# A decoder layer: k turned on VectorE instead of TensorE, x held back, and four steps moved in the order

## The chip, the cores and the metric

One core of a Trainium2 chip runs the whole program. The metric is the device time of one execution in microseconds. A core has TensorE (PE: products and transposes, which write PSUM), VectorE (DVE), ScalarE (ACT), GpSimd (POOL) and SyncE (SP). Each runs its own list of instructions in order, and they wait for each other by semaphores. SP, POOL and ACT can issue DMAs.

## The reference

One layer of a decoder with 512 prompt tokens and 32 sample tokens (8 sequences of 4). All is fp32.

```
h = rms_norm(x, g_pre);  z = h @ w_in                 # 1024 -> 3072 columns
q, k, v, ga, u, vs, gg = split(z)                     # 512, 256, 256, 512, 512, 512, 512
att = attend(q, k, v)          # prompt: causal attention; sample: the best past blocks of 256 keys
gm  = gelu(u) * (tril(w_sp) @ group_layer_norm(gelu(vs)) + b_sp)
y   = x + rms_norm(concat(att * silu(ga), gm * silu(gg)) @ w_out, g_post)
outputs: y, and the rows of k and v (token by token, 256 numbers each), prompt and sample
```

## The kernel before

Activations are held with channels on the partitions and tokens along the free dimension. The prompt's 512 tokens and the 32 sample tokens make five token tiles (four of 128, one of 32), columns 0 to 543 of `act_hi` and `act_lo`. Each fp32 factor is split into a high and a low part, and a product is the sum of hi x hi, lo x hi and hi x lo.

**Stages.** At the start the x tiles are loaded, normalised, turned on TensorE (`turn_x`) and split: ScalarE writes `act_hi` (semaphore `x_hi`), VectorE `act_lo` (`x_split`). The input projection then has 24 tiles of 128 columns, each in two halves over the tokens: 48 halves, numbered by h in `HALF_ORDER`. A half is 24 products. Its result lies in a Z bank until ScalarE or VectorE has taken it (step ZE). After half 47 come the sums for the output projection (MIX, Y, YS, Y2).

**The order.** `schedule()` (L82) writes one list by hand: half after half, and after each half the side steps that `after(h, ...)` has put there, in the order in which it was called. Every engine walks the same list and does its part of each step, so a step's place in the list is its place in every engine's queue. The steps of this case:

- WT and WB (L103, L104): the spatial weights turned, then one small product `rep` x `wspT`, for which VectorE writes `rep` in its part of WT (L1115).
- KVN (L100 to L102): k and v of a token tile, held as `kv32` (two tiles of k, two of v), turned on TensorE into a T bank (four turns, L1487), taken by ScalarE into `kvn`, and stored by POOL with two DMAs (L751, L752). v's part goes on into `v_st`.
- KTR: VectorE's 32x32 block transposes of the sample's cached K pages.
- VSN (L108, L116): the gelu'd `vs` turned, group sums and centring on VectorE, squares on ScalarE; LN and LNM finish the normalisation, LNM with a product on POOL.
- PSC, PN, PTR, PPV, ATT: one of 16 units of prompt attention (128 queries of a pair of heads): scores and maxima, exponentials and norms, turned probabilities, product with v, and the gate. Unit u starts after half 30 + u; PN is in the same half as PSC, PTR one half later, PPV and ATT two later.
- SP: the spatial product for a group pair, three of them after halves 43, 45 and 47 ahead of that half's PSC (L127).

**Banks.** Steps that turn something take the two T banks by turns; a step waits until the step two uses before has been read out (`bank_free`, L489). `pT_lo` on VectorE frees a bank of PTR, `vn` one of VSN, `sp_sum` one of SP.

**Queues.** SP issues x, the page table, one weight pair, K and V pages, `w_out` and the results. POOL issues the other weight pairs, `w_spatial`, the k and v stores, `g_sgu`, `b_spatial` and `g_post`, and between them computes half of the weights' low parts (`w_lo`, L696). `kv32` lies in the same memory as `zgg`, which VectorE writes from half 40 on (L1106).

Of the kernel before, what the change touches and what calls it, by code (L numbers as in the profile page):

```python
# [34 lines left out]
fp32 = mybir.dt.float32  # L35
# [7 lines left out]
P = 128  # L43
# [38 lines left out]
def schedule():  # L82

    s = [("XT", tt) for tt in range(TT)]
    side = {}

    def after(n, *steps):
        side.setdefault(n, []).extend(steps)


    for m, h in enumerate((3, 4, 5, 6, 10, 11, 12, 13, 15, 16, 17, 18, 21, 22, 23, 24)):
        after(h, ("KTR", m))
    after(6, ("WT",))
    after(7, ("WB",))
    after(9, ("DSC", 0), ("DSC", 1))
    after(12, ("KOW",))
    after(14, ("DSC", 2), ("DSC", 3), ("DOWN",))
    after(15, ("OWN",), ("DSM", 0))
    after(17, ("DEX", 0))
    after(16, ("KVN", 4), ("KVN", 0))  # L100
    for n, h in enumerate((17, 20, 22)):
        after(h, ("KVN", 1 + n))  # L102
    after(19, ("DPT", 0))  # L103
    after(20, ("DSC", 4), ("DSC", 5), ("DPV", 0, 0), ("DPV", 0, 1))  # L104
    after(22, ("DPV", 0, 2), ("DPV", 0, 3))
    after(24, ("DPV", 0, 4), ("DPV", 0, 5))
    after(28, ("DEX", 1))
    for n, h in enumerate((24, 25, 28, 29)):  # L108
        after(h, ("VSN", n))
    after(25, ("DSC", 6), ("DSC", 7), ("DPV", 0, 6), ("DPV", 0, 7))  # L110
    after(26, ("DOD", 0), ("DSM", 1))
    after(28, ("DOT", 0))
    after(30, ("DPT", 1))
    for pg in range(8):
        after(31 + pg // 2, ("DPV", 1, pg))
    after(31, ("VSN", 4))  # L116
    after(32, ("LN",))
    for n, tt in enumerate((4, 0, 1, 2, 3)):
        after(33 + 2 * n, ("LNM", tt))
    after(35, ("DOD", 1))  # L120
    after(36, ("DOT", 1))
    after(40, ("AS",))
    first = 30
    for h in range(first, 2 * NT):
        u = h - first
        if h in [2 * TILE_OF["gg", gp] + 3 for gp in range(3)]:
            after(h, ("SP", (h - 3) // 2 - TILE_OF["gg", 0]))  # L127
        if u < len(UNITS):
            after(h, ("PSC", u), ("PN", u))
        if 1 <= u < len(UNITS) + 1:  # L130
            after(h, ("PTR", u - 1))
        if 2 <= u < len(UNITS) + 2:
            after(h, ("PPV", u - 2))
# [13 lines left out]
    s += [("Y2", tt) for tt in Y_ORDER]  # L147
    return s
# [94 lines left out]
def build(nc, x_prompt, x_sample, cache_k, cache_v, page_table, g_pre, w_in, g_sgu, w_spatial,  # L243
# [8 lines left out]
    def kv_rows(prompt, sample, tt):  # L252
        if tt < 4:
            return prompt[0, 0, tokens(tt)].rearrange("s h d -> s (h d)")
        return sample[0].rearrange("b t h d -> (b t) (h d)")

    with ExitStack() as ctx:
        def sem(name):
            return ctx.enter_context(nc.semaphore(name))
# [9 lines left out]
        def place(name, shape, dt, at):  # L269
            return nc.alloc_sbuf_tensor_at(name, shape, dt, offset=at)  # L270
# [31 lines left out]
        y_sum = place("y_sum", [SMP, 2, 512], fp32, R_Q + 26624)  # L302

        R_V = region(4096 + 8192 + 10240)
        kvn = place("kvn", [P, 2, 512], fp32, R_V)
        ln_sq = place("ln_sq", [P, 512], fp32, R_V)
        g_sgu_bc = place("g_sgu_bc", [P, 512], fp32, R_V + 2048)
        w2_hi = place("w2_hi", [P, 2, D], f32r, R_V + 4096)
# [108 lines left out]
        k_in = [sem(f"k_in{n}") for n in range(4)]  # L417
        v_in = [sem(f"v_in{n}") for n in range(4)]

        stored_kv = [sem("stored_kv0"), sem("stored_kv1")]  # L420
        stored_kvs = sem("stored_kvs")
        stored, stored_sgu = sem("stored"), sem("stored_sgu")

# [142 lines left out]
        def _(sp):  # L566
# [86 lines left out]
            sp.wait_ge(stored, 16 * 2 * TT)  # L653
            sp.wait_ge(stored_sgu, 16)
            for n in range(2):
                sp.wait_ge(stored_kv[n], 2 * 32)
            sp.wait_ge(stored_kvs, 32)


# [1 line left out]
        def _(pool):  # L661
# [71 lines left out]
            for s in SCHEDULE:  # L733
                kind = s[0]
                if s == ("Z", TILE_OF["u", 0], 1):

                    pool.wait_ge(vst_done, 4)
                    pool.wait_ge(stored_kv[1], 2 * 32)
                    pool.dma_start(g_sgu_bc[:, :], g_sgu[0:1, :].broadcast_to([P, 512])).then_inc(gsgu_in, 16)
                elif kind == "Z" and next_split(*s[1:]) is not None:  # L740
                    n = next_split(*s[1:])
# [3 lines left out]
                        load_w_in((n + 3) // 2)  # L745
                elif kind == "KVN":
                    tt = s[1]
                    src = kvn[:, tt % 2, :] if tt < 4 else kv_s[:, :]
                    pool.wait_ge(t_free["act"], freed(T_FREED_BY, T_OF[s])[1])
                    landed = stored_kv[tt % 2] if tt < 4 else stored_kvs  # L750
                    pool.dma_start(kv_rows(k_prompt, k_sample, tt), src[:, 0:KVW]).then_inc(landed, 16)  # L751
                    pool.dma_start(kv_rows(v_prompt, v_sample, tt), src[:, KVW:2 * KVW]).then_inc(landed, 16)  # L752
                elif kind == "DOT" and s[1] == 1:

                    pool.wait_ge(dpv, 2 * PAGES)
# [25 lines left out]
        def _(act):  # L781
# [32 lines left out]
            for s in SCHEDULE:  # L814
# [72 lines left out]
                elif kind == "KVN":  # L887
                    n, tt = T_OF[s], s[1]
                    R = ROWS[tt]
                    if 2 <= tt < 4:  # L890
                        act.wait_ge(stored_kv[tt % 2], 32)
                        act.wait_ge(vst_done, tt - 1)
                    take(n, (kvn[:, tt % 2, :] if tt < 4 else kv_s[:, 0:512]), T[n % 2][0:R, :])
                    if tt < 4:
                        act.wait_ge(t_free["act"], freed(T_FREED_BY, n)[1])
                        nc.scalar.activation(v_st[:, tt, :, 0:HD], kvn[:, tt % 2, KVW:].rearrange("p (h d) -> p h d", h=KVH), ACT.Copy)\
                            .then_inc(vst_hi, 1)
                elif kind == "DEX":
                    r = s[1]
# [16 lines left out]
                elif kind == "VSN":  # L916
# [3 lines left out]
                    if tt:  # L920
                        act.wait_ge(ssq_done, tt)
                    else:
                        act.wait_ge(stored_kv[0], 2 * 32)
# [92 lines left out]
        def _(dve):  # L1016
# [32 lines left out]
            for s in SCHEDULE:  # L1049
# [19 lines left out]
                elif kind == "ZE":  # L1069
# [28 lines left out]
                    elif what in ("ga", "gg"):  # L1098
                        g = GATE_HALVES.index(h)
                        dst = zga if what == "ga" else zgg  # L1100
                        dve.wait_ge(z_hi, 12 + g + 1)
                        if g == 0:
                            dve.wait_ge(t_full, T_OF["VSN", 4] + 1)
                        if what == "gg" and j == 0 and half == 0:
                            dve.wait_ge(t_full, T_OF["KVN", 3] + 1)
                        nc.vector.scalar_tensor_tensor(dst[:, j, cols], th[:, g % 2, 0:wide], 1.0, bank[:, 0:wide], ALU.add, ALU.mult)\  # L1106
                            .then_inc(z_free["dve"], 1)
                elif kind == "WT":
# [8 lines left out]
                elif kind == "WB":  # L1117
# [3 lines left out]
                                            T[n % 2][0:SMP, 0:GRP * DEC_T].rearrange("p (g t) -> p g t", g=GRP).unsqueeze(2).broadcast_to([SMP, GRP, DEC_B, DEC_T]),  # L1121
                                            bd_mask[:, :, :].unsqueeze(1).broadcast_to([SMP, GRP, DEC_B, DEC_T]), ALU.mult)\
                        .then_inc(t_free["dve"], 1)
                elif kind == "KVN":
                    tt = s[1]
                    if tt < 4:
                        dve.wait_ge(vst_hi, tt + 1)
                        nc.vector.tensor_tensor(v_st[:, tt, :, HD:], kvn[:, tt % 2, KVW:].rearrange("p (h d) -> p h d", h=KVH),
                                                v_st[:, tt, :, 0:HD].bitcast(fp32), ALU.subtract).then_inc(vst_done, 1)
                elif kind == "KTR":  # L1130
                    m = s[1]
# [240 lines left out]
        def _(pe):  # L1372
# [47 lines left out]
            for s in SCHEDULE:  # L1420
# [4 lines left out]
                elif kind == "Z":  # L1425
# [6 lines left out]
                    if h < 3:  # L1432

                        pe.wait_ge(w_hi_done, t + 1)
                        pe.wait_ge(x_hi, 4)
                        if h == 2:
                            pe.wait_ge(xn_done, 2 * TT)
                        for k in range(KD):
                            mm(out, wh[:, k, :], act_hi[:, k, cols], start=(k == 0), stop=False)
                        if h == 1:  # L1440
                            turn_x(2)
# [254 lines left out]
```

## Time and profile before

| | us |
|---|---|
| median of three timed runs | 283.56 (283.49 to 284.8) |
| the profiled execution | 283.24 |
| its span in the trace | 281.5 |
| TensorE's products busy | 270.4 (96%) |
| VectorE busy | 197.4 (70%) |
| ScalarE busy | 154.9 (55%) |
| GpSimd busy | 81.5 (29%) |

Times in the trace count from the span's start. TensorE's granted clock is full (1.00, 2.4 GHz) until 275 us. Products are pipelined: a row shows one as 0.27 to 0.30 us long, but they start 0.12 to 0.13 us apart, so a wait is read from the idle time in brackets behind a row, or from the distance between starts. In a timeline row stand the start, the length of the group, engine, line, operation, out<-in, shapes, the count (xN), and the idle time of the engine before it with what ended it.

### The profile page before, as it was taken

Reading aid. Unit: us, or ns where it says so; the run is one execution under the profiler, and the core shown is the slowest. Engines: PE = TensorE matmul, PEld = TensorE weight load, DVE = VectorE, ACT = ScalarE, POOL = GpSimd, SP = SyncE. Lnnn points to the kernel's source line nnn. Section 1 sums busy time; section 2 is a strip of 40 time slices with the busy share of each in tenths; the row PEclk is TensorE's granted clock in tenths of the full one; section 3 lists DMA queues with packets and bytes.
Section 4 is the critical chain, followed back from the end, with each engine's and each line's share of the span. In section 5 each row is a group of like instructions: output and inputs, shape, how many; then the busy total and the mean of one; then the engine's idle time right before and its main releaser. Section 6 shows DMA issues by size and latency. Waiting matters only on the chain.

```text
span 281.5 us, 6112 instructions
## 1 busy us (share of the span) xinstructions
PE 270.4 (96%) x2155; PEld 237.5 (84%) x2155; DVE 197.4 (70%) x451; ACT 154.9 (55%) x355; POOL 81.5 (29%) x96
## 2 busy tenths in 40 slices
PE   8999999999999999999899999999899999999992
PEld 3799988999997887998787999998798976767892
DVE  4786885699743525835558889899979894927773
ACT  5973667632692323288875556555374563628621
POOL 4676505210412142243044373333350510000000
PEclk9999999999999999999999999999999999999998
DMA  7989994379999969530572017021008404040043
GB/s 246 332 270 196 207 282 114 125 206 232 265 313 283 318 190 311 152 122 31 149 242 68 2 29 234 1 81 71 0 2 275 193 1 149 2 150 2 19 175 123
DMA packets 29922, 43.39 MB, mean 154 GB/s; under 512 B 2963, under 2 KB 22419, under 8 KB 29892
## 3 DMA queue, kind: packets, MB, share of 16 engines
q1 hardware_dynamic: 26226, 29.76, 37.2%
q0 software_dynamic: 3664, 13.24, 15.0%
q8 instruction: 17, 0.28, 0.5%
q14 instruction: 13, 0.11, 0.1%
q10 hardware_dynamic: 2, 0.00, 0.0%
HBM read 39.59 MB, written 3.41 MB: 153 GB/s over the span
## 4 chain that ended last, share of the span: by engine, by line
PE 72%; DVE 14%; ACT 9%; issue 3%; DVEq 0%; POOL 0%; ACTq 0%; POOLq 0%
PE Z L1459 11%; PE Z L1464 10%; PE Z L1460 10%; PE T L1377 3%; DVE probs L1258 3%; PE S L1501 3%; PE Z L1415 2%; DVE pT_lo L1264 2%; PE O L1600 2%; PE O L1536 2%; PE S L1415 2%; PE S L1416 2%; PE Z L1417 2%; PE S L1417 2%; PE Z L1416 2%
## 5 line engine op out<-in xcount | busy, mean ns | idle before, releaser
L1459 PE MATMUL Z<-act_hi,w_hi 128*128 128x288 f32 (+1 forms) x344 | 89.5, 293 | 0.4 <-ACT zvs L873 0.3
L1460 PE MATMUL Z<-act_lo,w_hi 128*128 128x288 f32 (+1 forms) x344 | 88.0, 288 | 0.0
L1459 PEld LDWEIGHTS Z<-act_hi,w_hi 128*128 128x128 f32 x344 | 64.8, 188 | 2.6 <-issue 1.6
L1460 PEld LDWEIGHTS Z<-act_lo,w_hi 128*128 128x128 f32 x344 | 64.8, 188 | 0.0
L696 POOL TENSOR_TENSOR w_lo<-w_raw,w_hi 128x1024 fp32r<-128x1024 f32 x16 | 38.2, 2388 | 54.4 <-ACT w_hi L796 54.4
L1464 PE MATMUL Z<-act_hi,w_lo 128*128 128x256 f32 (+1 forms) x336 | 49.0, 288 | 0.0
L1464 PEld LDWEIGHTS Z<-act_hi,w_lo 128*128 128x128 f32 x336 | 44.8, 188 | 0.0
L796 ACT ACTIVATE w_hi<-w_raw 128x1024 fp32r<-128x1024 f32 x32 | 33.5, 1051 | 15.0 <-DMA w_raw<-in_w_out 10.0
L940 ACT ACTIVATE probs<-S,nmax 128x128 f32<-128x128 f32 (+3 forms) x32 | 16.6, 524 | 23.9 <-DVE nmax L1248 22.5
L1027 DVE TENSOR_TENSOR w_lo<-w_raw,w_hi 128x1024 fp32r<-128x1024 f32 x15 | 18.1, 1209 | 16.0 <-ACT w_hi L796 16.0
L1135 DVE STREAM_TRANSPOSE kT<-k_ring 128x1024 f32<-128x1024 f32 x16 | 19.7, 1238 | 0.4 <-PE S L1501 0.2
L704 POOL DMA_DIRECT2D w_raw<-in_w_in x10 | 9.3, 928 | 33.2 <-DVE w_lo L1027 29.7
L1258 DVE TENSOR_SCALAR probs<-probs,rsum 128x128 f32<-128x128 f32 (+3 forms) x32 | 15.2, 475 | 1.1
L1248 DVE TENSOR_REDUCE nmax<-S 128x1 f32<-128x128 f32 (+3 forms) x32 | 14.1, 480 | 1.2 <-PE S L1576 1.1
L1264 DVE TENSOR_TENSOR pT_lo<-T,pT_hi 128x128 fp32r<-128x128 f32 (+3 forms) x32 | 14.1, 482 | 0.1
L1377 PE MATMUL T<-ident,probs 128*128 128x128 f32 x80 | 12.1, 276 | 2.1 <-DVE vn L1227 0.9
L952 ACT ACTIVATE pT_hi<-T 128x128 fp32r<-128x128 f32 (+3 forms) x32 | 12.2, 440 | 0.0
L768 POOL TENSOR_TENSOR vn<-vn,g_sgu_bc 128x512 f32<-128x512 f32 (+1 forms) x5 | 6.4, 1285 | 19.4 <-DVE vn L1240 19.4
L1600 PE MATMUL O<-pT_hi,v_st 128*128 128x256 f32 x40 | 11.5, 315 | 0.5 <-DVE zga L1278 0.5
L777 POOL TENSOR_TENSOR zu<-zu,zgg 128x544 f32<-128x544 f32 x4 | 5.4, 1352 | 22.0 <-DVE zgg L1106 22.0
L882 ACT ACTIVATE th<-Z 128x256 f32<-128x256 f32 (+1 forms) x16 | 6.4, 399 | 9.7 <-PE Z L1464 9.5
L1255 DVE RECIPROCAL rsum<-psums 128x1 f32<-128x1 f32 x32 | 5.1, 160 | 8.9 <-ACT probs L940 8.9
(272 smaller groups left out, 557.3 us busy)
## 6 DMA issues: line engine op xcount, KB each, us to landing
w_raw<-in_w_in POOLq DMA_DIRECT2D x10, 1024.0 KB, 7.0
k_ring<-in_cache_k SPq DMA_DIRECT2D x64, 128.0 KB, 4.7
v_ring<-in_cache_v SPq DMA_DIRECT2D x64, 128.0 KB, 4.0
w_raw<-in_w_out SPq DMA_DIRECT2D x8, 512.0 KB, 4.4
x_sb<-in_x_prompt SPq DMA_DIRECT2D x4, 512.0 KB, 5.6
x_res<-in_x_prompt SPq DMA_DIRECT2D x4, 512.0 KB, 5.2
out<-y_sb SPq DMA_DIRECT2D x8, 256.0 KB, 2.0
w_raw<-in_w_in SPq DMA_DIRECT2D x2, 512.0 KB, 6.5
```

What stands on the lines that cost most here:

```text
L696: nc.gpsimd.tensor_tensor(w_split_tile(False, n), w_tile(n), w_split_tile(True, n).bitcast(fp32), ALU.subtract)\
L796: nc.scalar.activation(w_split_tile(True, n), w_tile(n), ACT.Copy).then_inc(w_hi_done, 1)
L940: ins = nc.scalar.activation(probs[:, u % 2, g, 0:keys], S[:, g * 512:g * 512 + keys], ACT.Exp, bias=nmax[:, u % 2, g:g + 1], accum_out=ps ...
L1027: nc.vector.tensor_tensor(w_split_tile(False, n), w_tile(n), w_split_tile(True, n).bitcast(fp32), ALU.subtract)\
L1135: nc.vector.transpose(kT[:, m // 2 % 2, m % 2, :, :, :].rearrange("p q a j -> p (q a j)"), k_slot(m).rearrange("p q c -> p (q c)")).then_i ...
L1258: nc.vector.tensor_scalar(part, part, rsum[:, u % 2, g:g + 1], 0.5, ALU.mult, ALU.mult).then_inc(p_norm, 1)
L1264: nc.vector.tensor_tensor(pT_lo[:, u % 2, 0:blocks, g, :], T[(n + g) % 2][:, 0:blocks * P].rearrange("p (j q) -> p j q", q=P), pT_hi[:, u ...
L1377: return nc.tensor.transpose(T[n % 2][0:out_rows, col:col + rows], in_, ident[0:rows, 0:rows])
L1459: mm(out, wh[:, k, :], act_hi[:, k, cols], start=(k == 0), stop=False)
L1460: mm(out, wh[:, k, :], act_lo[:, k, cols], start=False, stop=False)
L1464: last = mm(out, wl[:, k, :], act_hi[:, k, cols], start=False, stop=(k == KD - 1))
L1600: last = mm(O[o_bank(u)][:, 0:256], v_st[:, j, kvh, :], part[:, u % 2, j, :, :].rearrange("p g q -> p (g q)"), start=(j == 0 and e == 0), ...
```

## The change

- k of the four full token tiles is no longer turned on TensorE. In new steps KTB (after halves 22 and 23) VectorE transposes 32x32 blocks of the two k tiles in place; in KTD (after halves 34 and 35) POOL stores them with four DMAs each, in pieces of 32 numbers. VectorE's first write of `zgg` waits for these eight stores. v is still turned on TensorE, two turns for each full tile, and has a smaller tile `vn_t` of its own; the 32-token tile is as before.
- SP waits for x tile 1 before it issues x tiles 2 to 4 and what follows.
- The first products of halves 0 to 2 wait for three writes of `act_hi`, the fifth product for four.
- WB moves from half 7 to 8; VSN 2, 3, 4 from halves 28, 29, 31 to 27, 28, 29; in half 43 SP 0 goes behind PSC, and PPV ahead of PTR.
- With `kvn` gone from its memory, the load of `g_sgu` waits for nothing.

```diff
@@ schedule()
-    after(7, ("WB",))
+    after(8, ("WB",))
...
+    for j in range(2):
+        after(22 + j, ("KTB", j))
+        after(34 + j, ("KTD", j))
...
-    for n, h in enumerate((24, 25, 28, 29)):
+    for n, h in enumerate((24, 25, 27, 28)):
         after(h, ("VSN", n))
...
-    after(31, ("VSN", 4))
+    after(29, ("VSN", 4))
...
-        if h in [2 * TILE_OF["gg", gp] + 3 for gp in range(3)]:
-            after(h, ("SP", (h - 3) // 2 - TILE_OF["gg", 0]))
-        if u < len(UNITS):
-            after(h, ("PSC", u), ("PN", u))
...
+        spread = [gp for gp in range(3) if h == 2 * TILE_OF["gg", gp] + 3]
+        if spread and spread != [0]:
+            after(h, ("SP", spread[0]))
+        if spread == [0]:
+            after(h, ("PSC", u), ("SP", 0), ("PN", u), ("PPV", u - 2), ("PTR", u - 1))
+        else:
+            if u < len(UNITS):
+                after(h, ("PSC", u), ("PN", u))
...
@@ tiles and semaphores
-        kvn = place("kvn", [P, 2, 512], fp32, R_V)
+        vn_t = place("vn_t", [P, 2, KVW], fp32, R_V)
...
-        stored_kv = [sem("stored_kv0"), sem("stored_kv1")]
+        stored_v = [sem("stored_v0"), sem("stored_v1")]
+        stored_k, k_turned = sem("stored_k"), sem("k_turned")
@@ SP
             load_first(1)
+            sp.wait_ge(x_in[1], 16)
             for tt in (2, 3, 4):
                 sp.dma_start(x_sb[0:ROWS[tt], tt, :], x_src[tt]).then_inc(x_in[tt], 16)
@@ POOL
                 if s == ("Z", TILE_OF["u", 0], 1):
-                    pool.wait_ge(vst_done, 4)
-                    pool.wait_ge(stored_kv[1], 2 * 32)
                     pool.dma_start(g_sgu_bc[:, :], g_sgu[0:1, :].broadcast_to([P, 512])).then_inc(gsgu_in, 16)
...
+                    if tt < 4:
+                        pool.dma_start(kv_rows(v_prompt, v_sample, tt), vn_t[:, tt % 2, :]).then_inc(stored_v[tt % 2], 16)
+                    else:
+                        pool.dma_start(kv_rows(k_prompt, k_sample, tt), kv_s[:, 0:KVW]).then_inc(stored_kvs, 16)
+                        pool.dma_start(kv_rows(v_prompt, v_sample, tt), kv_s[:, KVW:2 * KVW]).then_inc(stored_kvs, 16)
+                elif kind == "KTD":
+                    j = s[1]
+                    rows = k_prompt[0, 0].rearrange("(b j) h d -> j b (h d)", j=32)
+                    pool.wait_ge(k_turned, j + 1)
+                    for a in range(4):
+                        at = P * j + 32 * a
+                        pool.dma_start(rows[:, :, at:at + 32], kv32[32 * a:32 * a + 32, j, 0:SEQ].rearrange("p (b i) -> p b i", i=32))\
+                            .then_inc(stored_k, 16)
@@ ScalarE
                     if 2 <= tt < 4:
-                        act.wait_ge(stored_kv[tt % 2], 32)
+                        act.wait_ge(stored_v[tt % 2], 16)
...
+                    if tt < 4:
+                        take(n, vn_t[:, tt % 2, :], T[n % 2][:, 0:KVW])
...
@@ VectorE
                         if what == "gg" and j == 0 and half == 0:
                             dve.wait_ge(t_full, T_OF["KVN", 3] + 1)
+                            dve.wait_ge(stored_k, 8 * 16)
...
+                elif kind == "KTB":
+                    j = s[1]
+                    dve.wait_ge(k_first, 2 * j + 2)
+                    nc.vector.transpose(kv32[:, j, 0:SEQ], kv32[:, j, 0:SEQ]).then_inc(k_turned, 1)
@@ TensorE
-                        pe.wait_ge(x_hi, 4)
...
                         for k in range(KD):
+                            if k % 4 == 0:
+                                pe.wait_ge(x_hi, 3 + k // 4)
                             mm(out, wh[:, k, :], act_hi[:, k, cols], start=(k == 0), stop=False)
...
-                    for j in range(4):
-                        last = turn(n, j * P, kv32[:, j, tokens(tt)], P, ROWS[tt])
+                    for j in range(4) if tt == 4 else (2, 3):
+                        last = turn(n, (j if tt == 4 else j - 2) * P, kv32[:, j, tokens(tt)], P, ROWS[tt])
```

## Rows read from the trace of the kernel before

**Rows 1.** TensorE's and others' busy time in one stretch; engine, us (instructions), clock, DMA.
```profile
165.00:203.00 38.00, 36.61 (x297) 34.45 (x295) 34.20 (x90) 21.23 (x59) 15.82 (x12) 1.00 0.24 77
```

**Rows 2.** Waits of TensorE; line waited for releaser: us in total, times, longest.
```profile
PE T L1377 <- DVE pT_lo L1264: 0.6, 1, 0.6
...
PE T L1610 <- DVE pT_lo L1264: 0.6, 1, 0.6
...
PE O L1600 <- DVE zga L1278: 0.5, 1, 0.5
```

**Rows 3.** Timeline at the start: start us, us, engine, line; and landings of x_sb.
```profile
9.43 1.07 ACT L824 ACTIVATE act_hi<-O 128x512 fp32r<-128x512 f32 x2
...
10.05 1.29 DVE L1059 TENSOR_TENSOR act_lo<-O,act_hi 128x512 fp32r<-128x512 f32 x2
...
10.65 1.18 PE L1439 MATMUL Z<-act_hi,w_hi 128*128 128x256 f32 x8 [0.54 <-ACT act_hi L824]
...
11.34 1.07 ACT L801 ACTIVATE x_sq<-x_sb 128x1024 f32<-128x1024 f32 x1
...
DMA to landing us min/median/max: 3.3/7.0/8.0
```

**Rows 4.** Timeline around WB, VectorE then TensorE.
```profile
38.63 0.17 DVE L1115 COPY rep<-ident 4x32 f32<-4x32 f32 x1
...
38.90 0.21 PE L1479 MATMUL T<-wspT,rep 4*32 4x32 f32 x2 [0.50 <-issue]
```

**Rows 5.** Timeline of TensorE, four turns and then two.
```profile
120.60 0.60 PE L1377 MATMUL T<-ident,zvs 128*128 128x128 f32 x4
...
121.04 0.38 PE L1377 MATMUL T<-ident,od 128*128 128x128 f32 x2
```

**Rows 6.** Groups of the page (count | busy, mean ns); timeline of VectorE.
```profile
L1135 DVE STREAM_TRANSPOSE kT<-k_ring 128x1024 f32<-128x1024 f32 x16 | 19.7, 1238 | 0.4 <-PE S L1501 0.2
...
104.78 0.69 DVE L1225 TENSOR_REDUCE ln_mu<-T 128x8 f32<-128x512 f32 x1 [4.98 <-PE T L1377]
```

**Rows 7.** Timeline, unit 0's second turn on TensorE and a VSN sum on VectorE.
```profile
136.09 0.30 PE L1377 MATMUL T<-ident,probs 128*128 128x128 f32 x1 [0.85 <-DVE vn L1227]
...
121.24 0.69 DVE L1225 TENSOR_REDUCE ln_mu<-T 128x8 f32<-128x512 f32 x1 [2.34 <-PE T L1377]
```

**Rows 8.** Timeline at half 43, VectorE twice, then TensorE.
```profile
202.63 0.68 DVE L1285 TENSOR_TENSOR sp_sum<-T,b_bc 128x512 f32<-128x512 f32 x1
...
203.96 0.75 DVE L1248 TENSOR_REDUCE nmax<-S 128x1 f32<-128x256 f32 x2
...
203.46 0.30 PE L1377 MATMUL T<-ident,probs 128*128 128x128 f32 x1 [0.60 <-DVE sp_sum L1285]
```

**Rows 9.** Timeline of POOL, halves 34 to 36.
```profile
153.35 2.37 POOL L696 TENSOR_TENSOR w_lo<-w_raw,w_hi 128x1024 fp32r<-128x1024 f32 x1 [2.05 <-ACT w_hi L796]
...
163.33 2.38 POOL L696 TENSOR_TENSOR w_lo<-w_raw,w_hi 128x1024 fp32r<-128x1024 f32 x1 [2.46 <-ACT w_hi L796]
...
166.27 0.94 POOL L704 DMA_DIRECT2D w_raw<-in_w_in  x1 [0.56 <-POOL w_lo L696]
...
167.20 1.25 POOL L757 DMA_DIRECT2D b_bc<-in_b_spatial  x2
```

**Rows 10.** Timeline of VectorE, three products of probs.
```profile
166.66 0.70 DVE L1258 TENSOR_SCALAR probs<-probs,rsum 128x384 f32<-128x384 f32 x1
...
188.20 0.42 DVE L1258 TENSOR_SCALAR probs<-probs,rsum 128x384 f32<-128x384 f32 x1
...
197.91 1.90 DVE L1258 TENSOR_SCALAR probs<-probs,rsum 128x128 f32<-128x128 f32 x1
```

**Rows 11.** DMA queues of the page; VectorE's first zgg in the timeline.
```profile
q1 hardware_dynamic: 26226, 29.76, 37.2%
...
q0 software_dynamic: 3664, 13.24, 15.0%
...
189.76 0.41 DVE L1106 SCALAR_TENSOR_TENSOR zgg<-th,Z 128x256 f32<-128x256 f32 x1
```

More of the change, by code:

```diff
@@ L125, in schedule @@
         u = h - first
-        if h in [2 * TILE_OF["gg", gp] + 3 for gp in range(3)]:
-            after(h, ("SP", (h - 3) // 2 - TILE_OF["gg", 0]))
-        if u < len(UNITS):
-            after(h, ("PSC", u), ("PN", u))
[L130 to L133, printed above, removed]
+        spread = [gp for gp in range(3) if h == 2 * TILE_OF["gg", gp] + 3]
[6 more added lines that the diff above has]
+                after(h, ("PSC", u), ("PN", u))
+            if 1 <= u < len(UNITS) + 1:
+                after(h, ("PTR", u - 1))
+            if 2 <= u < len(UNITS) + 2:
+                after(h, ("PPV", u - 2))
         after(h, ("ZE", h // 2, h % 2))
@@ L655, in _ @@
             for n in range(2):
-                sp.wait_ge(stored_kv[n], 2 * 32)
+                sp.wait_ge(stored_v[n], 2 * 16)
+            sp.wait_ge(stored_k, 8 * 16)
             sp.wait_ge(stored_kvs, 32)
@@ L747, in _ @@
                     tt = s[1]
-                    src = kvn[:, tt % 2, :] if tt < 4 else kv_s[:, :]
                     pool.wait_ge(t_free["act"], freed(T_FREED_BY, T_OF[s])[1])
-                    landed = stored_kv[tt % 2] if tt < 4 else stored_kvs
-                    pool.dma_start(kv_rows(k_prompt, k_sample, tt), src[:, 0:KVW]).then_inc(landed, 16)
-                    pool.dma_start(kv_rows(v_prompt, v_sample, tt), src[:, KVW:2 * KVW]).then_inc(landed, 16)
+                    if tt < 4:
[11 more added lines that the diff above has]
+                            .then_inc(stored_k, 16)
                 elif kind == "DOT" and s[1] == 1:
@@ L890, in _ @@
                     if 2 <= tt < 4:
-                        act.wait_ge(stored_kv[tt % 2], 32)
+                        act.wait_ge(stored_v[tt % 2], 16)
                         act.wait_ge(vst_done, tt - 1)
-                    take(n, (kvn[:, tt % 2, :] if tt < 4 else kv_s[:, 0:512]), T[n % 2][0:R, :])
+                    if tt < 4:
+                        take(n, vn_t[:, tt % 2, :], T[n % 2][:, 0:KVW])
+                    else:
+                        take(n, kv_s[:, 0:512], T[n % 2][0:R, :])
                     if tt < 4:
                         act.wait_ge(t_free["act"], freed(T_FREED_BY, n)[1])
-                        nc.scalar.activation(v_st[:, tt, :, 0:HD], kvn[:, tt % 2, KVW:].rearrange("p (h d) -> p h d", h=KVH), ACT.Copy)\
+                        nc.scalar.activation(v_st[:, tt, :, 0:HD], vn_t[:, tt % 2, :].rearrange("p (h d) -> p h d", h=KVH), ACT.Copy)\
                             .then_inc(vst_hi, 1)
@@ L922, in _ @@
                     else:
-                        act.wait_ge(stored_kv[0], 2 * 32)
+                        for n in range(2):
+                            act.wait_ge(stored_v[n], 2 * 16)
+                        act.wait_ge(vst_done, 4)
                     nc.scalar.activation(ln_sq[0:R, :], vn[0:R, tt, :], ACT.Square).then_inc(sq_done, 1)
@@ L1127, in _ @@
                         dve.wait_ge(vst_hi, tt + 1)
-                        nc.vector.tensor_tensor(v_st[:, tt, :, HD:], kvn[:, tt % 2, KVW:].rearrange("p (h d) -> p h d", h=KVH),
+                        nc.vector.tensor_tensor(v_st[:, tt, :, HD:], vn_t[:, tt % 2, :].rearrange("p (h d) -> p h d", h=KVH),
                                                 v_st[:, tt, :, 0:HD].bitcast(fp32), ALU.subtract).then_inc(vst_done, 1)
```

## The prediction

> **What bounds the kernel now.** I read the page's busy table first, then TensorE's waits, then the timeline at each wait. TensorE is the busiest engine, and its products follow each other without a break almost everywhere, so a microsecond of work or waiting taken from its queue is worth a microsecond unless something later waits anyway. The exception is halves 36 to 43: there VectorE is busy 34.20 of 38.00 us [rows 1], and two of TensorE's waits near 194 to 203 us, 0.6 us each, end on a T bank that VectorE's `pT_lo` still reads [rows 2]. In that stretch VectorE falls behind by about a unit and TensorE pays for it at its end. The reader is to see two regimes: a TensorE queue with a handful of holes, and one stretch where the hole's size is VectorE's lag.
>
> **The change, part by part.** All clock times are those of the profiled execution, 283.24 us long with a span of 281.5.
>
> *Start.* The first products wait for four `act_hi` writes; now the first four wait for three. The pair of writes runs from 9.43 for 1.07 us, so the third ends near 9.97; TensorE started at 10.65, 0.15 after the fourth ended at 10.50 [rows 3]. So the first product starts at about 10.12. But the second pass needs `act_lo`, which ends at 10.05 + 1.29 = 11.34 [rows 3]; with the same 0.15 that is 11.49, and it began near 10.65 + 1.03 = 11.68 (eight products in about 1.03 us before the next pass). Gain 0.2 us; bounds 0 and 0.5.
>
> *x held back.* SP now waits until x tile 1 has landed before it issues tiles 2 to 4, the page table and the second weight pair. Behind that wait in SP's queue stand all the K pages and everything later. ScalarE reads tile 2 at 11.34, straight after its own earlier work [rows 3]; the loads of x took 3.3 to 8.0 us from issue to landing [rows 3]. The two weight tiles stand ahead of x tile 2 in the queue either way, so I cost it at nothing; the cover is ScalarE's earlier work. Bounds: a gain of 0.2 (x tile 1 a little earlier) and a loss of 1.5, worked out below.
>
> *WB from half 7 to 8.* Its product waited for `rep`, which VectorE wrote at 38.63 for 0.17; TensorE stood idle 0.50 us before 38.90 [rows 4]. After half 8 `rep` is 2 us old. The next things due are the bank of half 6 and the second split, both done before 37. Gain 0.5 to 0.65; I take 0.6.
>
> *Eight turns leave TensorE.* Four full tiles need two turns each instead of four. Four turns take from 120.60 to 121.04, 0.44 us [rows 5]; four such pairs are 4 x 0.22 = 0.88 us, bounds 0.7 and 1.0. The turned copy on ScalarE halves too, off the path.
>
> *KTB on VectorE.* Two block turns of 128x512. Sixteen of 128x1024 took 1238 ns on average [rows 6]; half the columns cost 0.62 to 1.24 us, nearest 0.65. They come at halves 22 and 23, in front of the 4.98 us that VectorE idled before 104.78 [rows 6]: 1.3 us hidden. Without that cover they would cost 1.3.
>
> *Centring (VSN) at 27, 28, 29.* The transposes of unit 0 waited 0.85 us at 136.09 for the T bank that VSN 4 held [rows 7]. VSN 4 now runs two halves earlier, and that bank is long free. VSN 2 goes into the 2.34 us that VectorE idled before 121.24 [rows 7]; what follows it there keeps its order. About 2 us of VectorE and 0.6 of ScalarE also leave the stretch before unit 1's maxima, so `nmax` of units 1 and 2 comes sooner, and of the 0.5 us that O waited for `zga` [rows 2] I count 0.3. Gain 1.15; bounds 0.6 (VSN 4's old place taken by a wait for ScalarE's table loads) and 1.6.
>
> *SP 0 inside half 43.* Before, SP's sum (202.63, 0.68) and product stood ahead of unit 13's maxima (203.96) on VectorE, and TensorE's second turn of unit 12 waited 0.60 to 203.46 for that sum [rows 8]. Now the maxima go first: 0.67 us (two in 0.75, overlapping), so the sum ends near 204.0 and the turn waits until about 204.05. But PPV 11, 1.0 us of TensorE work that stood behind this turn, is now ahead of it. The next half starts 0.4 us sooner. Bounds -0.3 and 0.9.
>
> *k stored in 128-byte pieces.* Eight POOL DMAs of 512 pieces. One of 1024 pieces holds POOL for 0.94, two of 256 for 1.25 together [rows 9]; 512 lie between 0.63 and 0.94, nearest 0.72: 5.8 us. POOL is free from 153.35 + 2.37 = 155.7 to 163.33 [rows 9], 7.6 us in which only one 1.3 us `vn` product lies; queued behind are that product, the next `w_lo` (not needed before half 38) and a weight pair. Hidden on POOL. On VectorE not quite: a `probs` product of 384 columns took 0.70 us beside POOL's DMA issues and 0.42 at 188.20 without them [rows 10]. Six such VectorE instructions at +0.2 are 1.2 us; VectorE waits some 0.75 us for TensorE in these halves, so 0.4 is carried into the VectorE-bound stretch. Bounds 0 and 1.4.
>
> The page "SBUF — State Buffer" of the Trainium skill (section "Who interferes with whom") says that VectorE in a two-port mode and GpSimd lock each other out for a whole instruction. The 128-column `probs` at 197.91 agrees: 1.90 us, ending about when POOL's instructions do [rows 10]. By the rule each of the eight issues could block a VectorE instruction for its full length, which is a rival below; the 0.28 us above speaks for less.
>
> *The new wait for stored_k.* VectorE's first `zgg` (189.76 [rows 11]) waits for all eight stores; behind it stand every later step of VectorE, and through the T banks TensorE. 4096 pieces over 16 engines are 256 each. The mean packet of the SP queue took 0.372 x 16 x 281.5 / 26226 = 64 ns, that of POOL's 0.150 x 16 x 281.5 / 3664 = 184 ns [rows 11]. A piece between nothing and 184 ns makes 0 to 47 us from 155.7; nearest is the smaller packet: at most 16 us, so landed by 174. No cost; what hides it is the 34 us until 189.76.
>
> The page "DMA: Bandwidth & Descriptors" (section "Specifications") says that below 512 bytes a transfer is read, modified and written. No run here shows a piece of 128 bytes; if it doubled the 64 ns, the sum would stay as it is.
>
> **Sum.** 0.2 + 0.6 + 0.88 + 1.15 + 0.4 - 0.4 = 2.83 us; 283.24 - 2.83 = 280.4. The profiled run lies 0.3 under the median of the three timed runs (283.56), so this is 280.4 to 280.7; I say 280.4, since three bounds are wider towards gain.
>
> **Rivals.**
> *VectorE keeps what TensorE is given.* The lag in halves 36 to 43 is VectorE's own; if its units don't start earlier by what TensorE gains after half 30, the 1.15 and 0.4 come back as longer holes at 194 to 203. For it: 90% busy there [rows 1]. Against: VectorE enters the stretch waiting for TensorE, and VSN 4 leaves it. Time 283.24 - 1.68 + 0.4 = 282.0.
> *The lock in full.* Each of six VectorE instructions waits half an issue, 0.36: 2.2 us, less the 0.75 of slack: 1.4 instead of 0.4. Time 281.4.
> *x tile 2 comes late.* If it takes 8.0 us again, from an issue near 5.5 (x tile 1 landed), ScalarE reads it at 13.5 and not 11.34: 2.2 late, 0.7 of it slack; 1.5 lost, and the 0.2: 282.1. Against: it stood behind the same weights before.
> *The pieces are slow (the other side).* If a piece costs as much as a POOL packet, 184 ns, the stores end at 155.7 + 47 = 203, `zgg` is 13 us late and with it TensorE: 293. It decides from (189.76 - 155.7) / 256 = 133 ns a piece. For it: nothing so small is in the trace. Against: the smaller packets at 64 ns carry eight times the bytes.
> *The holes only move.* Another wait takes the place of WB's and VSN's: only the turns and the start remain, 282.2.
>
> **How the numbers follow.** Forecast 0.64 (its own range 279.2 to 281.6); VectorE keeps it 0.15; lock 0.07; late x 0.05; slow pieces 0.05; holes move 0.04. The best ends together (0.5 + 0.65 + 1.0 + 1.6 + 0.9) give 278.6. The range 278.8 to 282.2 leaves out slow pieces and a little at both edges. A measurement tells about 0.5%, 1.42 us, from no change, so faster means under 282.14: the forecast and the lock, most of the cases at 282.0 to 282.2 half and half: faster 0.82, same 0.13, slower 0.05.
>
> **What would show it.** No idle before `T<-wspT,rep`; two turns per full tile (twelve of kv, not twenty); the turns of unit 0 without a wait; TensorE's first product near 10.1; `zgg` not waiting on a DMA; half 44 some 2.8 us earlier; `probs` under 0.8 us beside the new DMA issues. It would be wrong if the holes at 194 to 203 grow by over a microsecond, if `zgg` waits for a store, or if ScalarE waits for x.

## The result, and the profile after

The changed kernel takes 280.91 us (median of six runs, 280.67 to 281.67) against 283.69 (283.49 to 285.0) beside it: a ratio of 0.9895 [0.9871, 0.9918], 2.78 us. The forecast was 280.4, range 278.8 to 282.2.

The profiled run of the changed kernel took 281.54 us (span 279.8) and lies above its own median, while that of before (283.24) lies below its own. So the two spans differ by 1.70 only. Cutting both traces at the starts of halves shows why (us from one start to the next, read on TensorE):

| from start to start | before | after | gained |
|---|---|---|---|
| span's start to half 3 (start) | 21.79 | 22.59 | -0.80 |
| 3 to 14 (WB) | 37.80 | 37.33 | 0.47 |
| 14 to 23 (KVN) | 37.24 | 36.35 | 0.89 |
| 23 to 34 (VSN) | 52.27 | 51.24 | 1.03 |
| 34 to 37 (KTD) | 16.59 | 16.84 | -0.25 |
| 37 to 42 | 25.13 | 25.11 | 0.02 |
| 42 to 44 (SP 0) | 13.79 | 13.38 | 0.41 |
| 44 to the end | 76.91 | 76.97 | -0.06 |

From half 3 to the end it is 259.73 and 257.22: 2.51 gained. This part hardly varies: in four kernels whose order behind half 3 is the same (the changed one, and the first, second and last of the experiments) it is 257.22, 257.31, 257.25 and 257.24. The start does vary: a run's time less 1.73 (what lies around the span) less this part gives half 3 at 21.7 to 22.7 in the six runs of the changed kernel, and at 22.0 to 23.5 in those of before. Effects of some tenths are therefore read below from half 3 on, in one trace each, and medians stand beside them. One execution of e3, 284.49 us, lies over 1.5% above that kernel's fastest and is left out of its row in the table of the experiments.

TensorE's waits after, the same view as [rows 2] (line, releaser: us in total, times, longest):

```profile
PE S L1431 <- DVE xn L1062: 1.4, 1, 1.4
PE T L1404 <- DVE sp_sum L1312: 0.9, 1, 0.9
PE T L1404 <- DVE pT_lo L1291: 0.6, 1, 0.6
PE T L1404 <- DVE vn L1254: 0.5, 1, 0.5
...
PE T L1404 <- DVE q_s L1243: 0.2, 1, 0.2
```

Of [rows 2], one wait on `pT_lo` and that on `zga` are gone; those on `vn` and `q_s` are new places, and the first is the start:

```profile
4.89 1.06 ACT L818 ACTIVATE x_sq<-x_sb 128x1024 f32<-128x1024 f32 x1 [1.73 <-DMA x_sb<-in_x_prompt]
...
7.31 0.66 PE L1431 MATMUL S<-ident,xn 128*128 128x128 f32 x4 [1.39 <-DVE xn L1062]
...
10.10 1.08 ACT L841 ACTIVATE act_hi<-O 128x512 fp32r<-128x512 f32 x2
...
10.84 0.36 PE L1467 MATMUL Z<-act_hi,w_hi 128*128 128x256 f32 x1
```

ScalarE first read x tile 0 at 4.89, at 4.16 before, though SP issued it at 0.82 in both and the change begins behind that issue. TensorE's first product is at 10.84, not at 10.1. Its place behind the writes of `act_hi` is the one that was meant: it starts 0.34 ahead of the end of the fourth write (11.18), where before it came 0.15 behind it. The writes themselves came 0.67 later than before.

WB (TensorE) has lost its wait:

```profile
41.94 0.24 PE L1507 MATMUL T<-wspT,rep 4*32 4x32 f32 x2
```

The k path, by the tile `kv` and its stores (count: shortest/median/longest ns; then the landing of the stores in us):

```profile
L1404 PE MATMUL T<-ident,kv x12: 270/272/273, 71.2 to 95.1; 128*128 128x128 f32 x8, 128*32 128x128 f32 x4
L768 POOL DMA_DIRECT2D out<-kv x8: 648/651/668, 154.1 to 158.6; - x8
...
L1150 DVE STREAM_TRANSPOSE kv<-kv x2: 669/686/703, 96.7 to 98.4; 128x512 f32<-128x512 f32 x2
...
DMA to landing us min/median/max: 2.1/2.2/3.5
```
```profile
188.36 0.41 DVE L1129 SCALAR_TENSOR_TENSOR zgg<-th,Z 128x256 f32<-128x256 f32 x1
```

Twelve turns, two block turns of 0.69 us, eight issues of 0.65, all landed before 163; `zgg` comes at 188.36 and waits for none. What the issues displace (POOL, then VectorE, then TensorE, answering [rows 9, 10]):

```profile
154.09 5.16 POOL L768 DMA_DIRECT2D out<-kv  x8
159.26 1.31 POOL L785 TENSOR_TENSOR vn<-vn,g_sgu_bc 128x512 f32<-128x512 f32 x1
```
```profile
154.08 0.29 DVE L1285 TENSOR_SCALAR probs<-probs,rsum 128x128 f32<-128x128 f32 x1
...
154.48 0.31 DVE L1285 TENSOR_SCALAR probs<-probs,rsum 128x128 f32<-128x128 f32 x1
...
157.24 0.68 DVE L1267 TENSOR_TENSOR vn<-vn,ln_rstd 128x512 f32<-128x512 f32 x1
...
159.76 0.97 DVE L1285 TENSOR_SCALAR probs<-probs,rsum 128x256 f32<-128x256 f32 x1
...
162.84 0.84 DVE L1243 COPY q_s<-T 64x32 f32<-64x32 f32 x4
```
```profile
163.83 0.41 PE L1404 MATMUL T<-ident,probs 128*128 128x128 f32 x2 [0.20 <-DVE q_s L1243]
```

The reader is to see that `probs` beside the issues is as short as ever (0.29, 0.31), that POOL's `vn` product, whose data VectorE finished at 157.92, starts at 159.26 behind the stores (1.34 us later; before it was 0.09), and that the `probs` which now meets it takes 0.97. The other product of that size, at 160.84, takes 0.35. `q_s` is then late and TensorE waits.

The centring (ScalarE, VectorE, TensorE, answering [rows 7]):

```profile
122.86 2.18 ACT L926 ACTIVATE pd<-S,bbias 128x128 f32<-128x128 f32 x8
...
125.09 0.68 ACT L946 ACTIVATE ln_sq<-vn 128x512 f32<-128x512 f32 x1
```
```profile
125.80 0.69 DVE L1257 TENSOR_REDUCE ln_var<-ln_sq 128x8 f32<-128x512 f32 x1 [3.28 <-ACT ln_sq L946]
...
127.98 0.67 DVE L1254 SCALAR_TENSOR_TENSOR vn<-ln_mu,T 32x512 f32<-32x512 f32 x1
```
```profile
128.71 0.66 PE L1404 MATMUL T<-ident,pd 128*128 128x128 f32 x4 [0.55 <-DVE vn L1254]
```

The 0.85 at 136.09 and the 0.5 at `zga` are gone. In their place ScalarE's square for VSN 3 stands behind eight exponentials, VectorE's variance waits 3.28 us for it, VSN 4's centring comes behind that, and TensorE waits 0.55 for the bank. SP 0 (VectorE, then TensorE, answering [rows 8]):

```profile
201.22 0.75 DVE L1275 TENSOR_REDUCE nmax<-S 128x1 f32<-128x256 f32 x2
201.89 0.68 DVE L1312 TENSOR_TENSOR sp_sum<-T,b_bc 128x512 f32<-128x512 f32 x1
```
```profile
202.71 0.30 PE L1404 MATMUL T<-ident,probs 128*128 128x128 f32 x1 [0.91 <-DVE sp_sum L1312]
```

One wait of 0.91 stands where two of 0.60 stood.

### The profile page after: what moved, and what is told of

The parts are those of the page before. It is cut to its first block, busy times and chain, and to the rows that moved or that the text cites. A ratio compares the mean times of both kernels' runs of the same rounds, so it can differ in the third digit from the quotient of the medians.

```text
span 279.8 us, 6103 instructions
## 1 busy us (share of the span) xinstructions
PE 269.2 (96%) x2147; PEld 236.6 (85%) x2147; DVE 199.0 (71%) x453; ACT 154.1 (55%) x355; POOL 84.3 (30%) x100
## 3 DMA queue, kind: packets, MB, share of 16 engines
q0 software_dynamic: 3728, 13.24, 15.3%
## 4 chain that ended last, share of the span: by engine, by line
PE 70%; DVE 16%; ACT 7%; issue 3%; DMA 1%; DVEq 0%; ACTq 0%
PE Z L1487 11%; PE Z L1492 10%; PE Z L1488 10%; PE T L1404 3%; DVE probs L1285 3%; PE O L1564 3%; PE S L1529 3%; PE Z L1442 2%; DVE pT_lo L1291 2%; PE S L1442 2%; PE S L1443 2%; PE Z L1444 2%; PE S L1444 2%; PE Z L1443 2%; PE O L1628 2%
## 5 line engine op out<-in xcount | busy, mean ns | idle before, releaser
L794 POOL TENSOR_TENSOR zu<-zu,zgg 128x544 f32<-128x544 f32 x4 | 5.4, 1356 | 21.7 <-DVE zgg L1129 21.7
```

## The experiments

All are edits of the changed kernel unless the text says otherwise; "from half 3" is from the start of half 3 to the end of the span.

| run | from half 3 | median (lowest to highest) | ratio to before |
|---|---|---|---|
| changed kernel | 257.22 | 280.91 (280.67 to 281.67) | 0.9895 [0.9871, 0.9918] |
| e1 no hold | 257.31 | 281.08 (280.69 to 282.85) | 0.9899 [0.9878, 0.9920] |
| e2 no split | 257.25 | 281.84 (281.01 to 282.02) | 0.9916 [0.9894, 0.9938] |
| e3 stores behind vn | 256.72 | 280.35 (280.07 to 281.80) | 0.9870 [0.9848, 0.9891] |
| e4 VSN 3 first | 257.05 | 280.54 (280.45 to 280.78) | 0.9882 [0.9863, 0.9902] |
| e5 k alone | 259.24 | 283.11 (282.60 to 285.23) | 0.9976 [0.9951, 1.0000] |
| e6 SP 0 old | 257.44 | 281.71 (281.57 to 283.61) | 0.9931 [0.9905, 0.9958] |
| e7 VSN old | 258.25 | 282.47 (281.63 to 285.07) | 0.9954 [0.9928, 0.9981] |
| e8 AS at 41 | 255.78 | 280.43 (279.30 to 282.35) | 0.9881 [0.9841, 0.9921] |
| e9 three orders | 255.34 | 279.81 (279.50 to 280.79) | 0.9851 [0.9823, 0.9879] |
| e10 w_lo first | 255.19 | 278.92 (278.60 to 280.46) | 0.9824 [0.9792, 0.9857] |
| e11 LN at 33 | 255.34 | 279.56 (278.88 to 281.62) | 0.9851 [0.9815, 0.9887] |
| e12 hold longer | 257.24 | 280.97 (280.79 to 281.36) | 0.9884 [0.9851, 0.9917] |

**The start: e1, e2, e12.**

```diff
-            sp.wait_ge(x_in[1], 16)
```


> The changed kernel, but SP no longer waits for x tile 1 before it issues tiles 2 to 4. In the profiled run of the changed kernel TensorE's first product began at 10.84 us and half 3 at 22.59, 11.75 later; before it was 10.65 and 21.79, 11.14 apart. Theory A (the hold costs nothing; x tile 0 merely landed later in that one run): 280.9 us within 0.3, and the distance stays 11.5 to 11.8. Theory B (the hold makes x tiles 2 and 3 late, and TensorE waits for them inside halves 0 to 2): the distance falls to about 11.1 and the time to 280.3. Theory C (the hold gives tiles 0 and 1 the road and so starts TensorE earlier): 281.4 or more.

```diff
-                            if k % 4 == 0:
-                                pe.wait_ge(x_hi, 3 + k // 4)
+                            if k == 0:
+                                pe.wait_ge(x_hi, 4)
```


> The changed kernel, but the first products of halves 0 to 2 wait for all four writes of act_hi again. Theory A (as predicted: the earlier first product is worth 0.2 us): 281.1. Theory B (the second pass waits for act_lo anyway, so the early start only opens a hole behind it): 280.9, the distance from the first product to half 3 shorter by what the first product starts later (0.2 to 0.5), half 3 where it was.

```diff
             sp.wait_ge(x_in[1], 16)
+            sp.wait_ge(w_first[0], 16)
```


> The changed kernel, but SP holds x tiles 2 to 4 until the first weight tile has landed as well (a larger dose of the same hold). In the changed kernel tiles 2 and 3 were issued from 6.31 us and ScalarE read tile 2 at 12.01 without a wait for it; ScalarE reads the first weight tile at 9.16. Theory A (the hold has slack, as predicted: ScalarE's earlier work covers it): ScalarE's read of x tile 2 waits at most 0.5 us, 280.7 to 281.2. Theory B (the rival in which x tile 2 comes late, priced at 1.5 us): issued near 8 us, x tile 2 is read at 13 or later, half 3 starts 1 to 2 us later than the 21.7 to 22.0 of undelayed starts, 281.9 or more.

e1 is theory A by its time (281.08); its profiled start was itself late (half 3 at 23.78, the distance 12.74, which no theory had); there ScalarE waited 0.73 us for x tile 2 without any hold. The larger dose is the clearer run:

```profile
7.65 0.82 SPq L628 DMA_DIRECT2D x_sb<-in_x_prompt  x2
...
11.64 1.07 ACT L819 ACTIVATE x_sq<-x_sb 128x1024 f32<-128x1024 f32 x1
```

Tiles 2 and 3 are issued at 7.65, in the kernel before from 2.83, and ScalarE still reads tile 2 at 11.64 with no wait: theory A. The x loads took 4.3 us at the median there, 7.0 in [rows 3]: issued later, they landed sooner behind their issue. The hold is free, and within these runs it gains nothing. In some traces ScalarE did wait for x tile 2, with the hold (0.41 in e6) and without it (0.36 in e5, 0.73 in e1), so such a wait is not the mark of the hold.

e2's median is 0.9 over the changed kernel, its lowest run 0.34; since a start varies by more than that, the times don't settle the split. The traces do, if they are read from the end of the fourth write of `act_hi`, which comes earlier or later with the loads. First e2, then e4 with the split (ScalarE, then TensorE):

```profile
9.57 1.07 ACT L841 ACTIVATE act_hi<-O 128x512 fp32r<-128x512 f32 x2
...
10.79 1.18 PE L1467 MATMUL Z<-act_hi,w_hi 128*128 128x256 f32 x8 [0.53 <-ACT act_hi L841]
...
13.71 1.12 PE L1467 MATMUL Z<-act_hi,w_hi 128*128 128x256 f32 x8
```
```profile
9.59 1.08 ACT L841 ACTIVATE act_hi<-O 128x512 fp32r<-128x512 f32 x2
...
10.32 1.18 PE L1467 MATMUL Z<-act_hi,w_hi 128*128 128x256 f32 x8
11.55 1.22 PE L1474 MATMUL Z<-act_lo,w_hi 128*128 128x256 f32 x8
12.61 1.11 PE L1477 MATMUL Z<-act_hi,w_lo 128*128 128x256 f32 x8
13.56 1.12 PE L1467 MATMUL Z<-act_hi,w_hi 128*128 128x256 f32 x8
```

From the end of the fourth write to the start of half 1 it is 3.07 us in e2 (10.64 to 13.71) and 2.89 in e4 (10.67 to 13.56). The three traces without the split have 3.06 or 3.07, the eleven with it 2.89 to 2.95. So the split gives about 0.17 by half 1: theory A, near its 0.2. The first product gains half a microsecond against that write, and most of it goes again in the wait for `act_lo`. Where ScalarE waits for no later x tile (before, e4, e7, e8, e12), halves 1 and 2 take 8.22 to 8.25 with or without the split, so half 3 keeps 0.13 to 0.16; in a late start it can't be told.

**The stores: e3, e5.** In e3, KTD is registered behind LNM:

```diff
-        after(34 + j, ("KTD", j))
...
         after(33 + 2 * n, ("LNM", tt))
+    for j in range(2):
+        after(34 + j, ("KTD", j))
```


> The changed kernel, but in half 35 POOL's vn product comes ahead of the second four k stores. Before, vn stood at 159.58 for 1.28 us and VectorE's probs of unit 5 came behind it (161.34, 0.35 us). In the changed kernel vn starts at 159.26, behind eight stores, 1.3 us after its data, and the 256-column probs beside it takes 0.97; TensorE then waits 0.35 at 163.5 for q_s. Theory A (the lag comes from the late vn product, not from the issues of the stores): vn near 158 again, probs 0.35 beside the second four stores, the wait for q_s gone, 280.6 (0.25 to 0.35 less). Theory B (VectorE is held by POOL's DMA issues themselves, 0.2 us each time): probs stays near 0.6 to 0.97 beside the stores, 280.9.

```profile
154.84 2.60 POOL L769 DMA_DIRECT2D out<-kv  x4
158.76 1.28 POOL L786 TENSOR_TENSOR vn<-vn,g_sgu_bc 128x512 f32<-128x512 f32 x1 [1.32 <-DVE vn L1268]
159.99 2.60 POOL L769 DMA_DIRECT2D out<-kv  x4
```
```profile
160.52 0.35 DVE L1286 TENSOR_SCALAR probs<-probs,rsum 128x256 f32<-128x256 f32 x1
...
160.98 0.44 DVE L1286 TENSOR_SCALAR probs<-probs,rsum 128x256 f32<-128x256 f32 x1
```

Theory A: beside four issues `probs` takes 0.35 and 0.44, and the stage from half 34 to 37 takes 16.63, 0.21 less; another 0.29 comes in half 42, 0.50 from half 3 on.

e5 is the kernel before with the k edits alone (the diff in the section on the change, without the start, WB, VSN and SP 0).

> The kernel before with the k change alone: two turns instead of four for each full token tile, KTB on VectorE, KTD on POOL; the start, WB, VSN and SP 0 as before. From the start of half 3 to the end the kernel before takes 259.73 us. Theory A (the terms add): eight turns less give 0.88, the vn product that the stores push into probs takes 0.24 back: 259.1 us from half 3, and 0.6 us under the time of before. Theory B (VectorE keeps what TensorE is given: the holes at 194 to 203 grow by as much): 259.5 to 259.7, and no difference that can be told.

Theory A by its stages: 36.39 against 37.24 from half 14 to 23 (0.85 gained), 16.80 against 16.59 from 34 to 37 (0.21 lost), none of it kept by VectorE later. The sum, 0.49, is under the 0.63 expected, because the stage of WB, which it doesn't touch, took 0.17 more in this trace: with WB in its old place TensorE waits again, 0.62 this time.

**The centring: e7, e4.**

```diff
-    for n, h in enumerate((24, 25, 27, 28)):
+    for n, h in enumerate((24, 25, 28, 29)):
...
-    after(29, ("VSN", 4))
+    after(31, ("VSN", 4))
```


> The changed kernel with VSN 2, 3, 4 back at halves 28, 29, 31. Theory A (the holes at 136.09 and 147.8 come back, the new one at 127.9 goes): 257.22 + 1.03 = 258.25 us from half 3, and about 1.0 over the changed kernel. Theory B (without them something else of ScalarE's table loads was the limit, so that less comes back): 257.5 to 257.8.

258.25: theory A. In e4, `after(28, ("DEX", 1))`, the step with the eight exponentials, stands behind the loop that places VSN.

> The changed kernel, but at half 28 VSN 3 stands ahead of DEX 1, so that ScalarE squares vn before its table load and the eight exponentials. In the changed kernel TensorE waits 0.55 us at 128.71 for VSN 4's centred vn (127.98), which VectorE makes only after VSN 3's variance (125.80, waiting 3.28 us for ScalarE's square behind the exponentials). Theory A (that queue order is the cause of the new hole): variance near 123.5, the hole at 127.9 shrinks from 0.82 to about 0.36, 280.4 to 280.5. Theory B (the exponentials become late instead, 0.7 us later, and TensorE waits for them at the first turns of the probabilities, 127.57): 280.9 or more.

```profile
121.77 0.64 ACT L946 ACTIVATE ln_sq<-vn 128x512 f32<-128x512 f32 x1 [1.00 <-DVE vn L1254]
```
```profile
145.98 0.36 PE L1628 MATMUL O<-pT_hi,v_st 128*128 128x256 f32 x1 [0.46 <-DVE zga L1305]
```

The cause is as theory A says: from half 3 on half 31 starts 0.74 earlier. But half 34 keeps 0.20 of that, for the wait on `zga` of [rows 2] is back (0.46): the next limit is the chain behind it. I had not named this third outcome.

**SP 0: e6.** The old order of half 43.

```diff
-        if spread and spread != [0]:
+        if spread:
             after(h, ("SP", spread[0]))
-        if spread == [0]:
-            after(h, ("PSC", u), ("SP", 0), ("PN", u), ("PPV", u - 2), ("PTR", u - 1))
-        else:
+        if True:
```


> The changed kernel with SP 0 and PPV of half 43 in the old order. The changed kernel takes 257.22 us from half 3 to the end. Theory A (as predicted, 0.4): 257.6, with two waits of TensorE (0.6 each) instead of one of 0.9. Theory B (both orders only place the same lag of VectorE): 257.2.

From half 42 to 44 it takes 13.77 against 13.38, 0.39: theory A at its place. From half 3 on only 0.22 is left: 0.08 lies behind half 44, which takes 76.90 there and 76.98 here, and the rest is some hundredths in other stages.

**What holds VectorE: e8, e10, and the better versions.**

```diff
-    after(40, ("AS",))
+    after(41, ("AS",))
```


> The changed kernel with AS (a product of 128x128 on VectorE) after half 41 instead of 40. In the changed kernel it takes 2.06 us at 183.25, beside POOL's w_lo (182.78 to 185.16); its like takes 0.29. TensorE's holes at 192.98 (0.87) and 201.53 (1.18) both end on a T bank that VectorE frees late. Theory A (VectorE's lag, made by such holds, sets the holes): AS takes about 0.3 in its new place, VectorE is up to 1.7 us earlier at half 41, the hole at 193 goes, and 256.0 to 256.6 us from half 3, 280.0 to 280.3 in all. Theory B (the hold only moves: w_lo holds the next product of probs instead): 257.2 and 280.9.

First the changed kernel, then e8: POOL's and VectorE's timeline, and a stretch of about halves 37 to 43 (columns as in [rows 1]):

```profile
182.78 2.38 POOL L706 TENSOR_TENSOR w_lo<-w_raw,w_hi 128x1024 fp32r<-128x1024 f32 x1 [1.87 <-ACT w_hi L813]
...
183.25 2.06 DVE L1333 TENSOR_TENSOR zga<-zga,q_s 128x128 f32<-128x128 f32 x1
```
```profile
163.40:201.40 38.00, 37.15 (x304) 35.27 (x302) 34.16 (x91) 21.23 (x59) 15.81 (x12) 1.00 0.25 77
```
```profile
187.85 0.28 DVE L1333 TENSOR_TENSOR zga<-zga,q_s 128x128 f32<-128x128 f32 x1
```
```profile
164.00:200.00 36.00, 35.90 (x298) 34.33 (x296) 32.02 (x89) 21.34 (x62) 15.09 (x11) 1.00 0.25 81
```

Theory A, and beyond it: 255.78, 1.44 less. The hole at 193 is gone and TensorE is busy 35.90 of 36.00. One 128x128 product had cost VectorE 1.8 us, and that was most of its lag at this hole. VectorE's busy share is about as before (32.02 of 36.00, 34.16 of 38.00): the share of [rows 1] didn't show what made the hole. The median falls by 0.48 only: three of the six runs took 281.2 or more, and none of these was traced. The medians of e9 to e11, which have the same move, lie 1.1 to 2.0 under the changed kernel. e9 is e3, e4 and e8 together.

> The changed kernel with three orders of the runs so far together: the second four k stores behind the vn product, VSN 3 ahead of DEX 1, AS after half 41. From half 3 to the end these gave 0.49, 0.17 and 1.44 us apart. Theory A (each shortens a hole of its own): 257.22 - 2.1 = 255.1. Theory B (0.29 of the first lay in the hole at 193 that the third takes away): 255.4. With a start of 21.7 to 22.0 that is 278.6 to 279.1 in all.

255.34: theory B; part of e3's gain lay in the hole that e8 takes away. e10 adds to e9:

```diff
-                    if lo_by(n) == "pool":
+                    if lo_by(n) == "pool" and n != TILE_OF["gg", 0] + 2:
                         split_lo(n)
...
                 elif kind == "ZE" and ORDER[s[1]][0] == "gg" and s[2] == 1:
                     j = ORDER[s[1]][1]
+                    if j == 0:
+                        split_lo(s[1] + 2)
```


> As the kernel with the three orders, but POOL makes the w_lo of the third gg tile ahead of its product zu<-zu,zgg of the first, not behind it. In the changed kernel with AS at 41 that w_lo ran from 193.70 to 196.10 and VectorE's 128-column probs beside it took 1.89 us (194.30), its like 0.29; w_hi was ready at 192.41. Theory A (the hold ends with POOL's instruction): w_lo ends near 194.8, probs takes about 0.6, VectorE is 1.2 us earlier at SP 0, TensorE's last hole in that stretch (0.86, on sp_sum) goes: 0.7 us less than with the three orders alone. Theory B (another probs is held instead, or zu comes late for SP 0): no less.

```profile
192.46 2.39 POOL L707 TENSOR_TENSOR w_lo<-w_raw,w_hi 128x1024 fp32r<-128x1024 f32 x1 [3.20 <-ACT w_hi L816]
194.81 1.36 POOL L797 TENSOR_TENSOR zu<-zu,zgg 128x544 f32<-128x544 f32 x1
```
```profile
194.26 0.67 DVE L1288 TENSOR_SCALAR probs<-probs,rsum 128x128 f32<-128x128 f32 x1
...
195.04 1.22 DVE L1288 TENSOR_SCALAR probs<-probs,rsum 128x128 f32<-128x128 f32 x1
```

Both theories in part: the first `probs` ends with `w_lo`, but the second is now held until `zu` ends (196.17). 0.15 less from half 3 on, not 0.7. e11 adds to e10 `after(33, ("LN",))` in place of 32.

> As the kernel before it, and LN (two table loads on ScalarE and two reciprocals on VectorE) after half 33 instead of 32. With VSN 3 first, TensorE waited 0.46 us at 145.98 for zga, behind a chain of ScalarE's table loads in which LN takes 137.94 to 139.56 and a load at 140.69; ScalarE sits idle 2.54 us at 144.6. Theory A (LN is what makes that chain late): the wait goes, 0.3 to 0.45 us less. Theory B (the loads only come in front of unit 3's exponentials, 0.5 us late there): no less.

Theory B by its time, though by other waits: half 34 starts earlier, but by half 37 TensorE has waited for `zga` (0.3) and `q_s` (0.4) instead, and 0.15 is lost. e10 has the lowest median, 278.92, 0.9824 of before, and 2.03 under the changed kernel from half 3 on.

## Why the prediction was right, and where not

The sum held because its largest terms were read off TensorE's own queue. Predicted and measured, from half 3 on 2.63 and 2.51 (half 44 comes 2.57 sooner behind half 3). The time itself was missed by 0.5, of which 0.45 is the base: I started from the profiled 283.24, and the median beside the result was 283.69.

- *Turns*, 0.88: 0.89. They were priced by starts of the same instruction, and nothing later took them back.
- *SP 0*, 0.4: 0.41, by the mechanism given: the maxima first, the sum after, PPV ahead of the waiting turn. What was not counted is that 0.07 comes back behind half 44, in every run with the new order.
- *WB*, 0.6: 0.47 in its stage. The wait is gone: the product starts 0.21 behind the one before it, where it was 0.80, and e5, with the old place, has the wait again. But 0.12 of the 0.59 came back by half 14, a few hundredths at a time; no run shows why.
- *Centring*, 1.15: 1.03. Here one step was missed: VSN 4 was moved forward, but the square of VSN 3 stays behind DEX 1 on ScalarE, so that VectorE and then TensorE wait at 127.9 (the hole is 0.82 against 0.36 there before). "That bank is long free" held for unit 0's turns; what the two steps between then wait for was not followed. More than 0.3 was gained at `zga` (0.48), which made up for some of it; that the sum came so near is partly luck. My low bound named ScalarE's table loads in this place.
- *Stores*, -0.4: -0.25, and for another reason. The failed step is "hidden on POOL": the `vn` product that "lies" in POOL's gap needs its place in it, and behind the eight issues it starts 1.34 us after its data, onto a `probs`. I had put the loss on the issues themselves (0.2 for each of six instructions); e3 shows them nearly free. The 0.70 in [rows 10] that I priced it by stands beside another DMA, and its size did not carry over: beside that same load's issue the `probs` takes 0.69 in the changed kernel and 0.42 in e3. That -0.25 lies near -0.4 is luck.
- *Slow pieces*, the other side: 2.2 us from issue to landing, 25 us before `zgg`. My 16 us was a bound by packets of other loads, and a piece is no packet: the queue shows 64 packets more (3728, before 3664) for 4096 pieces in place of 512 rows. The page "DMA: Bandwidth & Descriptors" of the Trainium skill (section "Anatomy of one DMA — SWDGE (gpsimd) path") gives 2.0 us plus the bytes over 436 GB/s, 2.15 for these 64 KB as an estimate. The trace agrees at the median (2.2, from 2.1 to 3.5).
- *KTB*, 0.65 each and hidden: 0.69, hidden. *The new wait*: none. *x held back*, 0: e12 shows the slack. *The start*, 0.2: 0.17 by half 1 and 0.13 to 0.16 by half 3, read from the last write of `act_hi`, and by the mechanism given. In the medians the start gave 2.78 - 2.51 = 0.27, which is less than starts vary.

The rival *VectorE keeps it* fell: the gain passes halves 37 to 42 unchanged (0.02). Most of VectorE's lag there came from holds beside POOL's products (e8), not from the time TensorE arrives. *The lock in full* was the right thing to watch but at the wrong instructions: the long holds are at POOL's products, not at its issues of the stores.

## What to carry to other kernels

Price a turn or a wait on the saturated engine from its own starts, and it holds; then follow each moved step through the engines it is queued on, for its new neighbours decide what comes back. When an engine's queue is given more work in a "free" gap, ask which instruction loses its slot and beside what it then runs. And before calling an engine the bound of a stretch, look there for single instructions several times as long as their like: moving one of them by one step here gained half as much as the whole change.

## What was not expected of the hardware

- A VectorE product of two SBUF tiles beside POOL's `w_lo` took 2.06 us, and 0.28 where it starts with POOL idle; a `probs` of 0.29 took 1.89 (194.30 in e8, beside `w_lo` from 193.70 to 196.10), and each such product ended within 0.2 us of POOL's. The page "SBUF — State Buffer" (section "Who interferes with whom") of the Trainium skill says that two SBUF inputs on VectorE contend with POOL's reads and that a two-port mode, which `tensor_scalar` can enter, blocks for the whole instruction. The product's rows agree with the first, and those of `probs` with the second, though no row shows its mode.
- POOL's issue of a store in 512 pieces took 0.65 us and held a `probs` of 0.35 by 0.09 at most.
- With one and the same program up to there, half 3 starts at 21.67 to 23.34 us in nine traces, the earliest ones those in which ScalarE waits for no x tile behind tile 0; what follows half 3 varies by 0.1 (four traces).
